# Two feed-forward layers on one core: output groups of 6, 8 and 8 hidden tiles in place of 8, 8 and 6, a third tile slot, and another order of loads, adds and operands

## The reference

```python
def swiglu(x, w_in, w_out):
    gu = x @ w_in
    gate, up = jnp.split(gu, 2, axis=-1)
    return (jax.nn.silu(gate) * up) @ w_out
...
        h = h + swiglu(rms_norm(h, norm_ffn[i]), ffn_w_in[i], ffn_w_out[i])
```

## Time and profile before

| | us |
|---|---|
| median of 3 runs | 3956.88 |
| lowest and highest | 3955.93, 3970.53 |
| profiled execution, its own time | 3954.32 |
| its span, first to last instruction | 3952.5 |
| busy in the span: PE | 3633.7 |
| busy in the span: PEld, DVE | 2866.2, 1938.1 |
| busy in the span: ACT, POOL | 1228.2, 1653.5 |

### The profile page before, as it was taken

One profiled execution on the slowest core, in us unless ns is written; L12 is line 12 of the kernel. 1 busy time (PEld: TensorE's weight loads), 2 busy tenths in 40 slices (PEclk: granted clock), 3 DMA queues, 4 the chain that ended last, 5 costly groups with the idle time before them and its releaser, 6 DMA issues. The chain is left out here.

```text
span 3952.5 us, 63280 instructions
## 1 busy us (share of the span) xinstructions
PE 3633.7 (92%) x25769; PEld 2866.2 (73%) x25769; DVE 1938.1 (49%) x2321; ACT 1228.2 (31%) x1641; POOL 1653.5 (42%) x1195
## 2 busy tenths in 40 slices
PE   7999999998999899988888799999899999887888
PEld 5776778886878577777777577888688778672667
DVE  5664665553243732236676337555522544159452
ACT  4452333331021642334545324333200320141221
POOL 2342477762323133333333226777333223373242
PEclk9999999999999999988898899999999999998999
DMA  2111122223211232321121111222321102100211
GB/s 92 41 44 40 32 85 80 80 98 102 85 62 37 80 124 96 117 75 61 46 77 45 54 67 59 82 82 80 133 91 44 58 32 85 49 1 1 86 43 69
DMA packets 72186, 268.09 MB, mean 68 GB/s; under 512 B 8000, under 2 KB 8384, under 8 KB 71488
## 3 DMA queue, kind: packets, MB, share of 16 engines
q1 hardware_dynamic: 66240, 244.37, 17.8%
q10 hardware_dynamic: 5760, 20.97, 1.3%
HBM read 204.49 MB, written 60.82 MB: 67 GB/s over the span
## 5 line engine op out<-in xcount | busy, mean ns | idle before, releaser
L150 PE MATMUL ps<-xh,whi 128*128 128x512 f32 x2048 | 659.9, 404 | 57.7 <-DVE xl L371 11.0
L117 POOL TENSOR_TENSOR gap<-ones 128x1 f32<-128x1 f32 x170 | 46.9, 276 | 1591.2 <-PE ps L150 1407.5
L150 PE MATMUL ps<-xl,whi 128*128 128x512 f32 x2048 | 651.3, 399 | 0.0
L150 PE MATMUL ps<-xh,wlo 128*128 128x512 f32 x2048 | 650.9, 399 | 0.0
L150 PEld LDWEIGHTS ps<-xh,whi 128*128 128x128 f32 x2048 | 387.1, 191 | 170.4 <-issue 19.1
L150 PEld LDWEIGHTS ps<-xl,whi 128*128 128x128 f32 x2048 | 390.5, 191 | 94.5
L150 PEld LDWEIGHTS ps<-xh,wlo 128*128 128x128 f32 x2048 | 390.0, 190 | 94.4
L120 POOL TENSOR_TENSOR wlo<-wraw,whi 128x1024 fp32r<-128x1024 f32 (+3 forms) x170 | 433.8, 2552 | 14.2
L799 PE MATMUL ps<-ffn_xh,whi 128*128 128x512 f32 x672 | 267.8, 399 | 12.6 <-DVE ffn_part L999 9.3
L799 PE MATMUL ps<-ffn_xl,whi 128*128 128x512 f32 x672 | 267.3, 398 | 0.0
L799 PE MATMUL ps<-ffn_xh,wlo 128*128 128x512 f32 x672 | 267.3, 398 | 0.0
(11 more groups left out here) (506 smaller groups left out, 6551.6 us busy)
## 6 DMA issues: line engine op xcount, KB each, us to landing
wraw<-w_ffn_in SPq DMA_DIRECT2D x88, 512.0 KB, 3.3
ffn_hidden<-sum_of_squares SPq DMA_DIRECT2D x44, 512.0 KB, 2.6
ffn_stage<-ffn_hidden SPq DMA_DIRECT2D x44, 512.0 KB, 3.3
rw_next<-rw_kept SPq DMA_DIRECT2D x40, 512.0 KB, 5.4
wraw<-w_ffn_out SPq DMA_DIRECT2D x32, 512.0 KB, 3.4
rw_kept<-rw_stage SPq DMA_DIRECT2D x24, 512.0 KB, 2.7
rw_kept<-rw_stage ACTq DMA_DIRECT2D x24, 512.0 KB, 2.7
wraw<-w_ple SPq DMA_DIRECT2D x16, 640.0 KB, 4.0
```

The lines of the kernel that those rows point to most:

```text
L117: nc.gpsimd.tensor_tensor(g.gap[:, 0:1], g.ones[:, 0:1], g.ones[:, 0:1], ALU.mult)
L150: last = nc.tensor.matmul(acc[:, hf, :], w[:, s, c:c + P], x[:, kt, hf * HALF:(hf + 1) * HALF], start=start and kt == 0 and n == 0, stop=s ...
```

## The change

In both layers:

- The output groups are 6, 8 and 8 tiles; the weights are packed on the host to match.
- `wsum`, which POOL's weight sums no longer need at the end, becomes a third slot of the tile ring. A load waits for the low of the tile three before it, not two.
- SP: load 2 goes ahead of the store of tile 20; pair 1 of group 0's weights goes ahead of the store of tile 21; pairs 2 and 3 and group 1's pair 0 stay behind load 13.
- DVE in the out part: the add of block 0 goes ahead of the lows of tiles 8 to 11, the add of block 1 ahead of those of 12 and 13. Tiles 20 and 21 use slots 6 and 7, which now belong to group 1, so their lows go between the last two adds of group 1, and group 1's last block marks its tiles as used, too.
- DVE in the head: `up_part` is released behind the T2 lows and no longer behind all twelve. The four T4 sums come next after the twelve lows and take one instruction each, with the raw T2 as operand in place of its high and low; `gate_sum` is released behind them; the T4 lows follow, and only then the scaling of the plain tile.
- ACT in the head: the highs of S1, A22, S4 and T4 and `first_part(1)` go ahead of the Silu of the plain tile. The loop body is unchanged, its first pass written out.

The diff, without the line that advances the semaphore counts and the one that names the third `tile_loaded` semaphore:

```diff
@@ -21,7 +21,7 @@
...
 KF = DFF // P
-FFN_GROUPS = (8, 8, 6)
+FFN_GROUPS = (6, 8, 8)
 RMS_EPS = 1e-6
...
@@ -669,6 +669,8 @@
...
         near_rstd = [g.ps[:, hf, :] for hf in (0, 1)]
+        ring = [stage[:, 0, :], stage[:, 1, :], wsum[:].rearrange("p a c -> p (a c)")]
+        RING = len(ring)
         lag4 = stage[:].rearrange("p a (b c) -> p (a b) c", c=HALF)
...
@@ -710,12 +712,14 @@
...
                 def load_tile(i):
-                    if i >= 2:
-                        sp.wait_ge(g.tile_low.sem, g.tile_low.base + i - 1)
+                    if i >= RING:
+                        sp.wait_ge(g.tile_low.sem, g.tile_low.base + i - RING + 1)
+                    elif i < 2:
+                        sp.wait_ge(g.t_low.sem, g.t_low.base + 16)
                     else:
-                        sp.wait_ge(g.t_low.sem, g.t_low.base + 16)
+                        sp.wait_ge(g.weight_low.sem, g.weight_low.base + PAIR * last_pair)
                     sp.wait_ge(g.hidden_stored.sem, g.hidden_stored.base + 16 * (i + 1))
-                    sp.dma_start(stage[:, i % 2, :], g.hidden_dram[i]).then_inc(g.tile_loaded[i % 2].sem, 16)
+                    sp.dma_start(ring[i % RING], g.hidden_dram[i]).then_inc(g.tile_loaded[i % RING].sem, 16)
 
...
@@ -727,15 +731,18 @@
...
                 load_blocks(sp, g, k_out[0], 0)
-                load_tile(0)
-                load_tile(1)
+                for i in range(RING):
+                    load_tile(i)
                 store(last_pair - 1)
-                for i in range(2, 8):
+                for i in range(RING, 8):
                     load_tile(i)
+                load_blocks(sp, g, k_out[0], 1)
                 store(last_pair)
...
                     load_tile(i)
-                stream_phase(sp, None, nc, g, k_out[0])
+                for q in range(2, KD // 2):
+                    load_blocks(sp, g, k_out[0], q)
+                load_blocks(sp, g, k_out[1], 0)
                 for i in range(FFN_SLOTS, KF):
...
@@ -859,7 +866,7 @@
...
                     wait_block(KD // 2 - 1, 1)
-                    out_block(grp, 1, kt_used=grp == 0, acc=banks(g, 2))
+                    out_block(grp, 1, kt_used=grp < 2, acc=banks(g, 2))
                 keep_busy(nc, g, 4, 22)
...
@@ -897,14 +904,14 @@
...
                 def tile_high(i):
-                    act.wait_ge(g.tile_loaded[i % 2].sem, g.tile_loaded[i % 2].base + 16 * (i // 2 + 1))
+                    act.wait_ge(g.tile_loaded[i % RING].sem, g.tile_loaded[i % RING].base + 16 * (i // RING + 1))
                     if i < FFN_SLOTS:
                         act.wait_ge(g.product_done.sem, prods(last_pair, i // 2))
-                    elif i < KF - 1:
-                        act.wait_ge(g.tile_used.sem, g.tile_used.base + tile_slot(i) + 1)
+                    elif tile_slot(i) == FFN_GROUPS[0] - 1:
+                        act.wait_ge(g.block_done.sem, first_out[0] + KD)
                     else:
-                        act.wait_ge(g.block_done.sem, first_out[0] + KD)
-                    nc.scalar.activation(hh[:, tile_slot(i), :], stage[:, i % 2, :], ACT.Copy).then_inc(g.tile_high.sem, 1)
+                        act.wait_ge(g.tile_used.sem, g.tile_used.base + tile_slot(i) + (1 if tile_slot(i) < FFN_GROUPS[0] else 0))
+                    nc.scalar.activation(hh[:, tile_slot(i), :], ring[i % RING], ACT.Copy).then_inc(g.tile_high.sem, 1)
 
...
@@ -926,19 +933,18 @@
...
                         t_high(n, i)
+                for n in (S1_, A22, S4_):
+                    weight_high(1, n, first_free)
+                for i in range(KD // 2):
+                    act.wait_ge(g.t_raw.sem, g.t_raw.base + KD // 2 + i + 1)
+                    t_high(T4_, i)
+                first_part(1)
                 act.wait_ge(g.gate_part.sem, g.gate_part.base + 2)
...
                 nc.scalar.activation(flat(banks(g, 0)), tmp.rstd, ACT.Copy).then_inc(g.near_ready.sem, 1)
-                weight_high(1, S1_, first_free)
-                weight_high(1, A22, first_free)
-                weight_high(1, S4_, first_free)
-                for i in range(KD // 2):
-                    act.wait_ge(g.t_raw.sem, g.t_raw.base + KD // 2 + i + 1)
-                    t_high(T4_, i)
-
-                with act.Fori(1, last_pair) as m:
+
+                def body(m):
                     free = lambda n: act.wait_ge(g.product_done.sem, prods(m, n))
-                    first_part(m)
                     weight_high(m, A11, free, 1)
...
@@ -948,6 +954,11 @@
...
                     weight_high(m, S4_, free, 1)
+
+                body(1)
+                with act.Fori(2, last_pair) as m:
+                    first_part(m)
+                    body(m)
                 first_part(last_pair)
...
@@ -979,8 +990,7 @@
...
                 def t4_sum(i):
-                    ch.link(dve, gained(t_raw[T4_][i], 2 * i + 1, slice(0, HALF), xh[:, T2_, i, :].bitcast(F32)))
-                    nc.vector.tensor_tensor(t_raw[T4_][i], t_raw[T4_][i], xl[:, T2_, i, :].bitcast(F32), ALU.subtract).then_inc(g.t_raw.sem, 1)
+                    gained(t_raw[T4_][i], 2 * i + 1, slice(0, HALF), t_raw[T2_][i]).then_inc(g.t_raw.sem, 1)
 
...
@@ -990,7 +1000,7 @@
...
                     dve.wait_ge(g.tile_high.sem, g.tile_high.base + i + 1)
-                    nc.vector.tensor_tensor(hl[:, at, :], stage[:, i % 2, :], hh[:, at, :].bitcast(F32), ALU.subtract).then_inc(g.tile_low.sem, 1)
+                    nc.vector.tensor_tensor(hl[:, at, :], ring[i % RING], hh[:, at, :].bitcast(F32), ALU.subtract).then_inc(g.tile_low.sem, 1)
 
...
@@ -1053,24 +1063,27 @@
...
                     t_sums(i)
-                for n in (T2_, T3_, T1_):
+                for i in range(KD // 2):
+                    t_low(T2_, i)
+                dve.sem_inc(g.up_part.sem, 2)
+                for n in (T3_, T1_):
                     for i in range(KD // 2):
                         t_low(n, i)
+                dve.wait_ge(g.t_low.sem, g.t_low.base + 12)
+                for i in range(KD // 2):
+                    t4_sum(i)
+                dve.wait_ge(g.t_raw.sem, g.t_raw.base + KD)
+                dve.sem_inc(g.gate_sum.sem, 2)
+                for i in range(KD // 2):
+                    t_low(T4_, i)
                 dve.wait_ge(g.rstd_ready.sem, g.rstd_ready.base + 1)
-                dve.wait_ge(g.t_low.sem, g.t_low.base + 12)
-                dve.sem_inc(g.gate_sum.sem, 2)
-                dve.sem_inc(g.up_part.sem, 2)
                 dve.wait_ge(g.block_done.sem, first + 1)
                 nc.vector.tensor_tensor(sg, flat(banks(g, 0)), tmp.rstd, ALU.mult).then_inc(g.gate_part.sem, 2)
-                for i in range(KD // 2):
-                    t4_sum(i)
                 dve.wait_ge(g.silu_ready.sem, g.silu_ready.base + 2)
...
                 nc.vector.tensor_tensor(hid, flat(banks(g, 2)), sg, ALU.mult).then_inc(g.half_ready.sem, 2)
-                for i in range(KD // 2):
-                    t_low(T4_, i)
                 dve.wait_ge(g.half_ready.sem, g.half_ready.base + 2)
...
@@ -1107,33 +1120,41 @@
...
                 hidden(m, 1)
-                for i in range(8, FFN_SLOTS):
+                add_to_h(dve, nc, g, first_out[0], 0, 0)
+                for i in range(8, 12):
                     tile_low(i)
-                with dve.Fori(0, KD // 2 - 1) as q:
+                add_to_h(dve, nc, g, first_out[0], 1, 0)
+                for i in range(12, FFN_SLOTS):
+                    tile_low(i)
+                with dve.Fori(1, KD // 2 - 1) as q:
                     for s in (0, 1):
...
                 add_to_h(dve, nc, g, first_out[0], 1, KD // 2 - 1)
-                for i in range(16, KF):
+                for i in range(16, 20):
                     tile_low(i)
-                for grp in (1, 2):
-                    if grp == 2:
-                        dve.wait_ge(g.hidden_stored.sem, g.hidden_stored.base + 16 * KF)
-                        clear_sum(dve, nc, g)
-                    with dve.Fori(0, KD // 2) as q:
-                        for s in (0, 1):
-                            add_to_h(dve, nc, g, first_out[grp], s, q)
-                            if grp == 2:
-                                sum_square(dve, nc, g, q, s, tmp.sq, KD)
+                with dve.Fori(0, KD // 2 - 1) as q:
+                    for s in (0, 1):
+                        add_to_h(dve, nc, g, first_out[1], s, q)
+                add_to_h(dve, nc, g, first_out[1], 0, KD // 2 - 1)
+                tile_low(20)
+                tile_low(21)
+                add_to_h(dve, nc, g, first_out[1], 1, KD // 2 - 1)
+                dve.wait_ge(g.hidden_stored.sem, g.hidden_stored.base + 16 * KF)
+                clear_sum(dve, nc, g)
+                with dve.Fori(0, KD // 2) as q:
+                    for s in (0, 1):
+                        add_to_h(dve, nc, g, first_out[2], s, q)
+                        sum_square(dve, nc, g, q, s, tmp.sq, KD)
...
```

(4 more changed lines are left out.)

## The result

| | before | after |
|---|---|---|
| median of 4 runs, us | 3962.20 | 3915.94 |
| lowest to highest | 3955.93 to 3970.53 | 3900.46 to 3918.93 |
| profiled execution, its span | 3952.5 | 3914.4 |
| feed-forward stretch, layer 0 | 718.3 | 697.9 |
| feed-forward stretch, layer 1 | 717.5 | 694.9 |

The ratio of the runs is 0.9874, with a 95% interval of 0.9840 to 0.9908: faster by 1.3%, 46 us by the medians. A second set of runs gave 0.9904, 38 us (experiment 11). The forecast was 3914 with a range of 3902 to 3934.

A forecast was written before the change was run, and what follows sets the result against it. PE is busy 3633.7 of 3952.5 us, so only its idle or lower-clock time at the feed-forwards' ends can go. Tails 15.9 + 15.4 and heads 6 + 6 make 43 us off 3956.9: 3914, range 3902 to 3934.

The forecast's parts named there:

- Sum: Both layers' tails and heads together: 15.9 + 15.4 + 6 + 6 = 43 us gained.
- Tail, what goes: Out part: PE's wait for POOL's weight split, its clock loss and tile 7's wait vanish, 18.4 and 17.9 us.
- The 0.8 us for tile 7: Block 0: PE's 0.8 us wait for tile 7's low goes, since group 0 has no tile 7.
- Tail, what comes: Block 3: new PE wait for block 1's add, queued on DVE behind four lows, taken as 2.5 us.
- Its bound without the third slot: Block 3: 6.9 us idle if loads keep today's pace, 8.4 with clock loss as the upper bound.
- Moving the 6 changes no sum: Output groups: moving the 6-tile group from last to first changes no sum.
- Third pair of weights: Tail: weights of q = 2 leave SP at about 918 to 924, needed split at 931, so nothing is late.
- Head: First pair of each layer: S4 starts earlier by 6 us, with bounds of 8.5 and nothing.
- The lock of the shared port: Head: DVE and GpSimd lock their shared port per instruction, which would give most of the head's gain back.
- rival 2: Head: DVE and POOL take turns throughout, so it gains at most 2 us: 3924 us, chance 0.14.
- Rival 3: Block 3: tile loads keep today's pace, 8.4 us lost there in each layer: 3926 us, chance 0.13.
- Rivals 4 and 5: Tail: group sizes alone act, 3968 us, chance 0.03; steady pairs: the early start upsets them, 3977 us, chance 0.03.

The follow-up runs named there:

- experiment 11: The changed kernel run again, unedited: 3915.9 us, ratio 0.9904 to the kernel before.
- Experiment 3: Changed kernel with the second weight pair put behind load 13 again: 3943.4 us, ratio 0.9962 to the kernel before.
- experiment 2: Changed kernel with output groups of 8, 8, 6: 3911.6 us, ratio 0.9873 to the kernel before.
- experiment 8: Changed kernel with gate_sum early, POOL held during T4 sums, scaling before T4 lows, block 1's add before tile 10's low: 3909.2 us, ratio 0.9876.
- Experiment 6: Changed kernel with POOL's lows of S1, A22 and S4 held until the T4 sums are done: 3930.8 us in one execution.
- experiment 4: Changed kernel with two tile slots in place of three: 3925.9 us in one execution.
- experiment 5: Changed kernel with gate_sum released early, beside up_part: 3916.2 us in one execution.
- experiment 7: Changed kernel with the plain tile's scaling ahead of the T4 lows on DVE: 3915.6 us in one execution.
- experiment 12: Changed kernel with the third weight pair ahead of load 11 and block 1's add ahead of tile 10's low: 3922.1 us in one run.

## Why the prediction was right, and where it was off

- *Sum.* 43 us were forecast from the trace, 43.0 is what the two stretches lost. That it fits so well is luck: the tails were forecast at 15.9 and 15.4 and gave 16.2 and 18.7, the heads at 6 and 6 and gave 4.3 and 3.9. In the profile of experiment 11 the same parts are 16.4, 14.3, 4.3 and 3.9, 38.9 in all. The medians say 46 and, in experiment 11's runs, 38.
- *Tail, what goes:* right in mechanism and size. Experiment 3 gives the wait back by the one place in SP's queue. The 18.4 and 17.9 us fit the tail without any new wait, 252.6: 271.7 - 252.6 = 19.1 and 271.3 - 252.6 = 18.7.
- *The 0.8 us for tile 7* were put down to group 0 having no tile 7. That was too narrow: with 8, 8, 6 and the third slot the wait is gone as well (experiment 2).
- *Tail, what comes:* the wait of block 3 for the add of block 1 was forecast at 2.5 us and measured at 2.7 and 0, again 2.5 and 2.5. In layer 0 two errors cancel in it: the last hidden tile was to be done 11.4 us after the first out matmul (907.2 - 895.8) and was done at 13.2, so the third slot saved 1.3 us there and not 3; from there to block 3 it took 14.9 us and not 16.3. Its bound without the third slot, 6.9, was measured at 6.2 and 6.6.
- *"Moving the 6 changes no sum":* right, and more than that: the 6 in front is what makes the wait for L637 possible, since block 3 then starts 25.2 us after block 0 and not 33.6. The change's name names the part that costs a little.
- *Third pair of weights "leaves SP at about 918 to 924, needed, split, at 931":* right (917.6), but only because block 3 waits: split at 927.9, the weights were ready 1.3 us before block 4 began, and without the wait for L637 they would have been late by 1.4 (experiment 8).
- *Head:* forecast at 6 us, measured at 4.3 and 3.9. The term that was mis-sized is the T4 sums: the prediction took A12 at 485.4, between 484.2 and 488.4, by the argument that POOL had only three lows left. It had more: the low of A12 was held up beside DVE's lows and ended at 483.4, and the low of S3 followed before those three. All four sums met POOL, at 1.67 us each; A12 came 38.5 us from the first plain matmul, where 485.4 is 36.1 from it (449.26), so 2.4 us later, behind 6.1 us of wait where 3 to 4 was named as the sign. In the other direction the T4 lows were cheaper (3.35 us, not the middle of 2.7 and 5.8), and A22 kept its clock, with only 0.24 us of idle before it.
- *The lock of the shared port:* rival 2 had the mechanism, and its price was about right for the sums and wrong for the whole, because POOL's work there is finite. Experiment 6 shows the cost moving from the sums to the lows (4.65 and 5.74) instead of vanishing. What the Trainium skill (SBUF — State Buffer, section SBUF: two separate sides) says of a lock held for a whole instruction agrees with these rows and with the 6.67 us.
- *Rival 3*, the tile loads at the old pace, is what experiment 4 comes near with two slots; the third slot keeps it away.
- *Rivals 4 and 5:* no run showed either. The steady pairs are as before, PE busy for 360 of 360 us.

Left open: why the tile loads before the last store go out sooner in some executions, which then show no wait for L637; what the new order of the adds brings by itself; and how the 4 us of the head divide among its edits, since of these only two were changed alone (experiments 5 and 7).

## What to carry to other kernels

When a stage ends and another begins, list for each in-order queue what the new stage needs first, and put that ahead of anything that waits for the old stage's last result; here one pair of loads ahead of one store was worth 24 of 39 us by one profile and 28 of 43 by another. A wait shown by the profile is the last of several paths: before removing it, work out where the next one ends, or the idle time only moves (experiment 5), or a wait that it covered comes to light (experiment 8). And judge a change of a few us by the stretch it touches, not by the whole time.

## What the runs showed of the hardware that was not expected

The code between the two feed-forwards is the same in all kernels, but it took from 1194.5 us (experiment 8) to 1215.6 us (experiment 12). PE's waits in it sum to 116.8 and 119.6 us, so they explain 3 of the 21. The windows of these stretches, with the columns of the earlier trace rows:

```profile
1147.00:2342.00 1195.00, 1077.49 (x14250) 865.72 (x14250) 570.28 (x803) 482.06 (x606) 377.81 (x264) 0.94 0.21 74
```

```profile
1144.00:2360.00 1216.00, 1095.79 (x14251) 879.88 (x14251) 572.54 (x802) 482.92 (x606) 378.76 (x264) 0.92 0.20 73
```

PE is busy 18 us longer with the same matmuls, at a granted clock of 0.92 instead of 0.94. This stretch has many short gaps, and how many of its matmuls run at 1.2 GHz and not 2.4 differs from one execution to the next. That is where most of the scatter between runs can come from (18 us from the lowest to the highest of the changed kernel); the feed-forward, whose long middle has no gap, repeats far better: of the ten tails without a wait nine took 252.6 us and one 252.7.

The same idle time does not always cost the same clock, either. In the changed kernel 6.1 us before A12 were followed by this window:

```profile
489.00:493.60 4.60, 4.55 (x11) 3.68 (x12) 4.48 (x5) 1.08 (x2) 2.71 (x2) 0.53 0.36 114
```

The 2.2 us before S2 in the kernel before had it as well (0.58), while the 2.7 us for L637 did not: the tail of layer 0 is 3.0 us above the floor, the wait and almost nothing more. But that is this one execution. In layer 1 of experiment 11 the same kernel waits 2.5 us at the same place, and behind it stands this window:

```profile
2818.16:2825.00 6.84, 6.63 (x22) 5.26 (x23) 3.74 (x4) 1.74 (x2) 2.71 (x3) 0.75 0.43 160
```

The tail is then 4.4 us above the floor. So a wait of 2.5 to 2.7 us for L637 costs 0.3 us beyond itself or about 1.8: the tail is 255.3 to 255.6 us in four of the layers that have it and 256.9 to 257.0 in five others, experiment 5 having one of each.

And DVE and POOL do not simply take turns. In the changed kernel DVE's lows from 476.3 to 482.2 kept their 0.68 us each while POOL needed 8.76 for two subtractions, 7.1 of them for the first (the later ones of this head took 1.3 to 1.7 each), and right behind them the four sums took 1.67 each:

```profile
476.27 8.76 POOL L759 TENSOR_TENSOR wlo<-wraw,whi 128x512 fp32r<-128x512 f32 x2 [6.70 <-ACT whi L891]
485.00 1.71 POOL L759 TENSOR_TENSOR wlo<-ffn_wsum,whi 128x512 fp32r<-128x512 f32 x1
```

What decides which of the two is held up was not tried.
